# A two-layer hybrid trunk in one program: squares summed on VectorE, the norms' odd tiles on VectorE, three waits placed elsewhere

## The chip, the cores and the metric

The kernel runs on one core of a Trainium2 chip. The metric is the device time of one execution in microseconds (us). The core has TensorE (PE, matrix products), VectorE (DVE), ScalarE (ACT), GpSimd (POOL) and SyncE (SP, which here only issues loads). Each engine works through its own instruction list in order, and engines wait for each other on semaphores.

## The reference

Two layers over 512 latent and 256 context tokens of width 1024, in float32. Each layer:

```
h      = rms_norm(x) * gain * (1 + scale) + shift          # scale, shift from silu(c) @ w_mod
qa,ka,va,qb,kb,vb,qkv,z,beta,a,gate = split(h @ w_in)
o_a    = attention(rms(qa), rms(ka), va)                   # with rotary columns
o_b    = neighbourhood_attention(qb, kb, vb)               # 8 x 16 window, learned bias
o_c    = gated_delta(conv(qkv), beta, a) * silu(z)         # both directions, chunks of 64 tokens
x      = x + gate_m * ((sum_n sigmoid(gate_n) * (o_n @ w_branch[n])) @ w_out)
x      = x + gate_f * (square(relu(h2 @ w_ffn1)) @ w_ffn2) # h2: norm and modulation again
```

The second layer keeps only the latent tokens after its token mixers. A last rms_norm ends the trunk.

## The kernel before

Activations lie transposed: channels on the 128 partitions, tokens along the free dimension, so x is `xT`, eight tiles (k = 0 to 7) of 128 channels by 768 tokens (512 where only latent tokens count). Every product of float32 data is done as three TensorE passes over a high and a low half (`hh`, `hl` for activations, `wh`, `wl` for weights; lines 423 to 425). SP loads weight slots into a ring of three; `high` (line 1001, ACT) copies a slot to `wh`, and `split` (line 1686, POOL) makes `wl`. `high(l, name, i)` works two slots ahead, and before each slot it waits until the product that used the place three slots earlier has been filled. PSUM is four buffers used in turn by `take`: the fourth product after one needs that one's buffer emptied.

The program is one hand-written order for each engine. In a layer it goes: norm "mix"; twelve conv projections and z; the delta rule (six steps `s`, two directions `d`, each with five steps of a matrix power series, whose product is written L554); q and k heads (six `j`, each a square, its sum by TensorE at L808, root, reciprocal, and two projections `x = 2j, 2j+1` of the neighbourhood branch between); attention; 24 gate and branch products `x` whose sum is merged into `mT`; eight `out` products; norm "ffn"; eight groups of ff1 and ff2. After the second layer there is a norm "fin". So five norms run in all: three over 768 tokens (mix of both layers, ffn of the first) and two over 512 (ffn of the second, fin).

A norm has two parts.

- *The sum of squares.* ACT squares tile k (L957) into one of two buffers, and TensorE multiplies it by a matrix of ones and adds up over k (L600): eight products, each buffer free for the next square when its product has run. ACT then takes the root (L959) and DVE the reciprocal (L1260).
- *Scaling.* For even k, DVE multiplies x by gain and reciprocal root into `ht` (L1282, one piece for latent and one for context tokens), ACT adds the shift and rounds to `hh` (L976), DVE writes the remainder `hl` (L1291). For odd k, POOL multiplies x by the root (L1696), ACT applies gain and shift (L981) and rounds (L984), and DVE writes `hl` (L1296). `ht` has three buffers. In "fin" POOL takes tiles 1, 3 and 5, and DVE the rest.

In the residual stretch ahead of a norm, DVE adds product j into `xT[:, j]` (`residual`, L1621) and so frees the product's PSUM buffer. ACT's list there is: all `high` calls of the stretch first, then the norm's root table and its squares.

The delta state's zeroing (L1460) waits for `z_saved`, the store of z to DRAM that shares the place, and stands on DVE ahead of the first decay (L1468) and masked matrices (L1476, L1480); L1487 makes the first X out of them, and L1502 and L1506 empty the products of the power series.

After gate and branch product 23, DVE multiplies (L1603) and adds (L1606); ACT rounds all eight tiles of `mT` (L1226) and DVE writes their remainders (L1613), tile by tile ahead of the first `out` product.

Of the kernel before, what the change touches and what calls it, by code (L numbers as in the profile page):

```python
# [15 lines left out]
F32 = mybir.dt.float32  # L16
# [90 lines left out]
def program(nc, a, out, x_store, skew, bias_rows, z_store, book):  # L107
    book["final"] = book.get("final", False)
    with ExitStack() as ctx:
# [108 lines left out]
        def want_out(l, t):  # L218
            return l == 0 or t < LT

# [189 lines left out]
        def _(pe):  # L410
# [184 lines left out]
            def norm(l, which, ntok):  # L595
                ps = take(pe, "ss", l, which)
                for k in range(KC):
                    pe.wait_ge(*act_done.at("sq", l, which, k))
                    for t0, t1 in ((0, LAT), (LAT, TOK))[:1 if ntok == LAT else 2]:
                        last = mm(ps[:, t0:t1], ones, sq_n[:, k % 2, t0:t1], start=(k == 0), stop=(k == KC - 1))  # L600
                    if k < KC - 1:
                        last.then_inc(*pe_done.mark("ss", l, which, k))
                last.then_inc(*filled("ss", l, which))
# [338 lines left out]
        def _(act):  # L942
            A = nc.scalar.activation

            def norm(l, which, ntok):
                act.wait_ge(*dve_done.at("eps"))
                A(small[:, 62:63], eps[:, 0:1], ACT.Sqrt)
                for k in range(KC):

                    if l == 0 and which == "mix":  # L950
                        if k == 0:
                            act.wait_ge(*read("x", TT - 1))
                    else:
# [18 lines left out]
                for k in range(KC):  # L972
                    if k % 2 == 0:
                        act.wait_ge(*dve_done.at("scaled", l, which, k))
                        for t0, t1, c in spans(ntok):
                            A(hh[:, k, t0:t1], ht[:, k % 3, t0:t1], ACT.Identity, bias=modcs[:, l, 24 * w + k, c:c + 1])\  # L976
                                .then_inc(*act_done.mark("hhi", l, which, k))
                    else:
                        act.wait_ge(*pool_done.at("hx", l, which, k))
                        for t0, t1, c in spans(ntok):  # L980
                            A(ht[:, k % 3, t0:t1], ht[:, k % 3, t0:t1], ACT.Identity, scale=gains[:, l, w, k, c:c + 1],  # L981
                              bias=modcs[:, l, 24 * w + k, c:c + 1]).then_inc(*act_done.mark("aff", l, which, k))
                        act.wait_ge(*act_done.at("aff", l, which, k))
                        A(hh[:, k, 0:ntok], ht[:, k % 3, 0:ntok], ACT.Copy).then_inc(*act_done.mark("hhi", l, which, k))  # L984
# [24 lines left out]
            for l in range(DEPTH):  # L1009
# [164 lines left out]
                for j in range(6):  # L1174
# [3 lines left out]
                    A(asq[:, 0:n], qk[:, j, 0:n], ACT.Square).then_inc(*act_done.mark("asq", l, j))  # L1178
                    act.wait_ge(*full("ass", l, j))
# [43 lines left out]
                for k in range(KC):  # L1223

                    act.wait_ge(*dve_done.at("merge", l, 23))
# [28 lines left out]
        def _(dve):  # L1254
            V = nc.vector

            def inverse_root(l, which, ntok):
# [4 lines left out]
            def norm(l, which, ntok):  # L1262
# [13 lines left out]
                for k in range(KC + 1):  # L1276
                    if k < KC and k % 2 == 0:

                        if k >= 3:
                            dve.wait_ge(*dve_done.at("h", l, which, k - 3))  # L1280
# [90 lines left out]
            for l in range(DEPTH):  # L1371
                nt = TOK if l == 0 else LAT
                pcol, modc = pcols[:, l, :], modcs[:, l, :, :]
                if l == 0:
# [4 lines left out]

                    inverse_root(0, "mix", TOK)  # L1380
# [78 lines left out]
                dve.wait_ge(*z_saved.at(l))  # L1459
                V.memset(state[:, 0, :, :], 0.0).then_inc(*dve_done.mark("S0", l))  # L1460
# [135 lines left out]
                for k in range(4):  # L1596
                    branch_low(l, 2, k)
                for x in range(24):
                    n, dc = divmod(x, 8)
                    dve.wait_ge(*full("br", l, x))  # L1600
# [10 lines left out]
                for k in range(KC):  # L1611
                    dve.wait_ge(*act_done.at("mhi", l, k))
                    V.tensor_tensor(hl[:, k, 0:nt], mT[:, k, 0:nt], hh[:, k, 0:nt].bitcast(F32), ALU.subtract)\  # L1613
                        .then_inc(*dve_done.mark("mlo", l, k))
# [35 lines left out]
        def _(pool):  # L1650
# [39 lines left out]
            def normed(l, which, ntok, ks=range(1, KC, 2)):  # L1690

                pool.wait_ge(*dve_done.at("rs", l, which))
                for k in ks:
                    if k >= 3 and which != "fin":
                        pool.wait_ge(*dve_done.at("h", l, which, k - 3))
# [5 lines left out]
            for l in range(DEPTH):  # L1701
# [8 lines left out]
                if l == 0:  # L1710
                    normed(l, "mix", TOK, (1,))
                for p in range(2):
                    split(l, "c", c_order[p])
                normed(l, "mix", TOK, (3, 5, 7) if l == 0 else (1, 3, 5, 7))

                pool.wait_ge(*pool_done.at("hx", l, "mix", KC - 1))
# [190 lines left out]
                normed(l, "ffn", nt)  # L1907
# [38 lines left out]
```

## Time and profile before

| | us |
|---|---|
| median of three runs | 3248.0 |
| lowest, highest | 3242.76, 3248.76 |
| the profiled execution's own time | 3252.78 |
| its span | 3251.0 |
| PE busy | 2994.1 |
| DVE busy | 1231.6 |
| ACT busy | 1060.5 |
| POOL busy | 1071.1 |

The mean granted TensorE clock is 0.968 of full speed.

The profile describes one execution; a row gives start, duration, engine, source line and tiles. "R" is the one large scratch tensor in which most work buffers lie, `xT`, `ht` and the squares among them. Busy shares are means over stages with different limits, so what a stage waits for has to be read at its own place in the trace.

### The profile page before, as it was taken

Reading aid. Unit: us, or ns where it says so; the run is one execution under the profiler, and the core shown is the slowest. Engines: PE = TensorE matmul, PEld = TensorE weight load, DVE = VectorE, ACT = ScalarE, POOL = GpSimd, SP = SyncE. Lnnn points to the kernel's source line nnn. Section 1 sums busy time; section 2 is a strip of 40 time slices with the busy share of each in tenths; the row PEclk is TensorE's granted clock in tenths of the full one; section 3 lists DMA queues with packets and bytes.
Section 4 is the critical chain, followed back from the end, with each engine's and each line's share of the span. In section 5 each row is a group of like instructions: output and inputs, shape, how many; then the busy total and the mean of one; then the engine's idle time right before and its main releaser. Section 6 shows DMA issues by size and latency. Waiting matters only on the chain.

```text
span 3251.0 us, 57566 instructions
## 1 busy us (share of the span) xinstructions
PE 2994.1 (92%) x24931; PEld 2500.1 (77%) x24931; DVE 1231.6 (38%) x1754; ACT 1060.5 (33%) x1770; POOL 1071.1 (33%) x720
## 2 busy tenths in 40 slices
PE   5997888998889999799999979999999899989998
PEld 3886777776668888688888868788777688768886
DVE  3773433244541212322222258654235621232223
ACT  3542222225542112322221235433225532243222
POOL 3233344220313333222222322355330344444442
PEclk7998999999999999899999989999999999999999
DMA  6115453110002232121222221100310034323331
GB/s 229 53 35 176 149 184 107 54 44 7 11 23 59 67 99 72 33 66 60 64 65 65 61 69 52 47 3 4 84 49 11 11 91 133 101 71 93 96 97 59
DMA packets 303690, 231.93 MB, mean 71 GB/s; under 512 B 16784, under 2 KB 275280, under 8 KB 302544
## 3 DMA queue, kind: packets, MB, share of 16 engines
q1 hardware_dynamic: 297360, 204.58, 21.0%
q0 software_dynamic: 3776, 17.91, 1.5%
q10 hardware_dynamic: 2304, 5.77, 0.5%
q8 instruction: 198, 3.24, 0.4%
q14 instruction: 52, 0.43, 0.0%
HBM read 217.22 MB, written 11.98 MB: 71 GB/s over the span
## 4 chain that ended last, share of the span: by engine, by line
PE 79%; DVE 10%; issue 5%; ACT 4%; DMA 1%; POOL 1%; ACTq 0%; DVEq 0%; POOLq 0%
PE ps L423 20%; PE ps L424 20%; PE ps L425 20%; PE ps L554 5%; DVE stat L1316 2%; PE ps L508 2%; PE ps L529 2%; DVE R L1428 1%; PE ps L546 1%; DVE R L1282 1%; PE ps L435 1%; PE ps L600 1%; PE ps L770 1%; PE ps L720 1%; ACT R L878 1%
## 5 line engine op out<-in xcount | busy, mean ns | idle before, releaser
L1686 POOL TENSOR_TENSOR wl<-wring,wh 128x1024 fp32r<-128x1024 f32 (+1 forms) x312 | 721.1, 2314 | 1339.8 <-ACT wh L1001 1339.8
L423 PE MATMUL ps<-hh,wh 128*128 128x512 f32 (+1 forms) x2560 | 923.4, 361 | 73.7 <-DVE hl L1291 41.2
L424 PE MATMUL ps<-hl,wh 128*128 128x512 f32 (+1 forms) x2560 | 905.1, 354 | 0.0
L425 PE MATMUL ps<-hh,wl 128*128 128x512 f32 (+1 forms) x2560 | 904.3, 353 | 0.0
L423 PEld LDWEIGHTS ps<-hh,wh 128*128 128x128 f32 x2560 | 489.9, 191 | 163.1 <-issue 57.6
L424 PEld LDWEIGHTS ps<-hl,wh 128*128 128x128 f32 x2560 | 491.0, 192 | 68.2 <-issue 5.1
L425 PEld LDWEIGHTS ps<-hh,wl 128*128 128x128 f32 x2560 | 490.2, 191 | 66.2
L1001 ACT ACTIVATE wh<-wring 128x1024 fp32r<-128x1024 f32 (+1 forms) x312 | 307.7, 987 | 522.8 <-PE ps L425 497.8
L1621 DVE SCALAR_TENSOR_TENSOR R<-ps,modcs,R 128x512 f32<-128x512 f32 x216 | 136.3, 659 | 388.4 <-PE ps L425 387.5
L424 PE MATMUL ps<-fl,wh 128*128 128x512 f32 (+1 forms) x768 | 274.8, 358 | 0.0
L425 PE MATMUL ps<-fh,wl 128*128 128x512 f32 (+1 forms) x768 | 274.5, 357 | 0.0
L423 PE MATMUL ps<-fh,wh 128*128 128x512 f32 (+1 forms) x768 | 274.3, 357 | 0.0
L554 PE MATMUL ps<-R 64*64 64x64 f32 x5376 | 184.8, 224 | 23.9 <-issue 7.9
L554 PEld LDWEIGHTS ps<-R 64*64 64x64 f32 x5376 | 171.1, 138 | 39.9 <-issue 21.8
L1603 DVE TENSOR_TENSOR R<-ps,R 128x768 f32<-128x768 f32 (+1 forms) x48 | 39.6, 824 | 410.1 <-PE ps L425 410.1
L1635 DVE TENSOR_TENSOR R<-R 128x768 f32<-128x768 f32 (+1 forms) x64 | 53.9, 841 | 363.0 <-ACT R L1239 363.0
L878 ACT ACTIVATE R<-ps,stat 128x768 f32<-128x768 f32 (+2 forms) x160 | 116.0, 728 | 143.8 <-DVE stat L1316 139.8
L423 PEld LDWEIGHTS ps<-fh,wh 128*128 128x128 f32 x768 | 144.7, 188 | 23.7
L424 PEld LDWEIGHTS ps<-fl,wh 128*128 128x128 f32 x768 | 144.5, 188 | 23.3
L425 PEld LDWEIGHTS ps<-fh,wl 128*128 128x128 f32 x768 | 144.4, 188 | 23.3
L529 PE MATMUL ps<-R 128*64 128x128 f32 x1408 | 95.2, 279 | 38.2 <-DVE R L1337 29.3
L1239 ACT ACTIVATE R<-ps 128x768 f32<-128x768 f32 (+1 forms) x64 | 45.2, 706 | 255.1 <-PE ps L425 198.3
(236 smaller groups left out, 3775.6 us busy)
## 6 DMA issues: line engine op xcount, KB each, us to landing
wring<-in_w_ffn SPq DMA_DIRECT2D x128, 512.0 KB, 3.9
wring<-in_w_in SPq DMA_DIRECT2D x116, 512.0 KB, 3.8
wboth<-in_w_mod SPq DMA_DIRECT2D x80, 512.0 KB, 6.4
wring<-in_w_branch SPq DMA_DIRECT2D x48, 256.0 KB, 2.7
wring<-in_w_out SPq DMA_DIRECT2D x16, 512.0 KB, 4.2
x_store<-R POOLq DMA_DIRECT2D x2, 3072.0 KB, 9.0
R<-x_store POOLq DMA_DIRECT2D x2, 3072.0 KB, 11.6
R<-in_w_mod SPq DMA_DIRECT2D x7, 512.0 KB, 13.4
```

The source lines that it names most:

```text
L423: mm(ps[:, t0:t1], ahk, rh[:, k, t0:t1], start=(k == 0), stop=False)
L424: mm(ps[:, t0:t1], ahk, rl[:, k, t0:t1], start=False, stop=False)
L425: last = mm(ps[:, t0:t1], alk, rh[:, k, t0:t1], start=False, stop=(k == kn - 1))
L508: last = mm(ps[u][:, c0:c0 + n1 - n0], q[lo:lo + HD, t * P:t * P + P], k[lo:lo + HD, n0:n1], start=True, stop=True)
L529: mm(PS[3][HD * u:HD * u + HD, 512:512 + P], vt[b][:, c0:c0 + HD], probT[br][:, u, b, :], start=(b == 0), stop=(b == nk - 1))
L554: last = mm(out[lo:lo + HALF, h * HALF:h * HALF + HALF], left[lo:lo + HALF, h, :], right[lo:lo + HALF, h, :], start=True, stop=True)
L878: nc.scalar.activation(prob[br][p % 2][:, u, 0:n], score_ps(l, p)[u][:, 0:n], ACT.Exp, bias=stat[:, sl, 0:1], accum_out=stat[:, sl, 1:2])\
L1001: A(slot_view(wh, n % NSPL, *slot), w, ACT.Copy).then_inc(*act_done.mark("whi", *slot))
L1316: V.tensor_reduce(stat[:, sl, 0:1], ps[:, 0:n], AX.X, ALU.max, negate=True)\
L1621: V.scalar_tensor_tensor(out=xT[:, j, t0:t1], in0=pair(*key)[:, t0:t1], scalar=modc[:, gate + j, c:c + 1], in1=xT[:, j, t0:t1], op0=ALU.mu ...
L1635: V.tensor_tensor(f, f, f, ALU.mult).then_inc(*dve_done.mark("fsq", l, j))
L1686: G.tensor_tensor(slot_view(wl, n % NSPL, l, name, i), w, slot_view(wh, n % NSPL, l, name, i).bitcast(F32), ALU.subtract)\
```

## The change

Six edits, all of them in what stands on which engine and in which order:

1. The squares of tiles 0 to 5 are added up on VectorE (`square_sum`, five additions per norm), each put behind a residual; TensorE multiplies by ones only this sum and tiles 6 and 7. The squares of tiles 1 to 5 and 7 lie in the three `ht` buffers.
2. In "mix" and "ffn" VectorE multiplies the odd tiles too (L1299 of the new file), and POOL none.
3. The delta state's zeroing moves behind the first masked matrices.
4. The square of head j+1 stands on ACT between the two projections of head j, where it stood behind both (`head_square`).
5. ACT rounds tile k of `mT` once merge 16+k is done, and no longer waits for merge 23 in all eight.
6. DVE writes the remainder of tile 0 of `mT` ahead of merge 23.

```diff
+        def square_home(k):
+            return sq_n[:, k // 6, :] if k in (0, 6) else ht[:, k % 3, :]
...
             def norm(l, which, ntok):                         # TensorE
-                for k in range(KC):
-                    pe.wait_ge(*act_done.at("sq", l, which, k))
+                for k in (KC - 3, KC - 2, KC - 1):
+                    pe.wait_ge(*(dve_done.at("sum", l, which, k) if k == KC - 3 else act_done.at("sq", l, which, k)))
+                    sq = sq_n[:, 0, :] if k == KC - 3 else square_home(k)
...
-                    if k >= 2:                                # ScalarE
-                        act.wait_ge(*pe_done.at("ss", l, which, k - 2))
-                    A(sq_n[:, k % 2, 0:ntok], xT[:, k, 0:ntok], ACT.Square).then_inc(*act_done.mark("sq", l, which, k))
+                    if k in (4, 5, 7):
+                        act.wait_ge(*dve_done.at("sum", l, which, k - 3))
+                    A(square_home(k)[:, 0:ntok], xT[:, k, 0:ntok], ACT.Square).then_inc(*act_done.mark("sq", l, which, k))
...
-                        act.wait_ge(*pool_done.at("hx", l, which, k))
+                        act.wait_ge(*dve_done.at("scaled", l, which, k))
...
+                head_square(l, 0)
+                for j in range(6):
...
+                        if x == 2 * j + 1 and j < 5:
+                            head_square(l, j + 1)
...
-                    act.wait_ge(*dve_done.at("merge", l, 23))
+                    act.wait_ge(*full("gate", l, 23))
+                    act.wait_ge(*dve_done.at("merge", l, 16 + k))
...
+            def square_sum(l, which, ntok, k):                # VectorE
+                dve.wait_ge(*act_done.at("sq", l, which, k))
+                dve.wait_ge(*(dve_done.at("sum", l, which, k - 1) if k > 1 else act_done.at("sq", l, which, 0)))
+                V.tensor_tensor(sq_n[:, 0, 0:ntok], sq_n[:, 0, 0:ntok], square_home(k)[:, 0:ntok], ALU.add)\
+                    .then_inc(*dve_done.mark("sum", l, which, k))
...
+                    if k < KC and k % 2:
+                        V.tensor_tensor(ht[:, k % 3, 0:ntok], xT[:, k, 0:ntok], rs_n[:, 0:ntok], ALU.mult)\
+                            .then_inc(*dve_done.mark("scaled", l, which, k))
...
-                dve.wait_ge(*z_saved.at(l))
-                V.memset(state[:, 0, :, :], 0.0).then_inc(*dve_done.mark("S0", l))
...
                 for d in range(2):
                     delta_keys(l, 0, d)
+                dve.wait_ge(*z_saved.at(l))
+                V.memset(state[:, 0, :, :], 0.0).then_inc(*dve_done.mark("S0", l))
...
                     residual(("out", l, j), j, 16)
+                    if 2 <= j < KC - 1:
+                        square_sum(l, "ffn", nt, j - 1)
...
                             residual(("ff2", l, g - 1, j), j, 40)
+                            if g == NG and 2 <= j < KC - 1:
+                                after = (1, "mix", TOK) if l == 0 else (DEPTH, "fin", LAT)
+                                square_sum(*after, j - 1)
...
-                normed(l, "ffn", nt)                          # GpSimd
```

VectorE at the first layer's `out` products, before. Each residual is two pieces, 512 and 256 tokens; ps_full is the product it waits for, and the rows shown are residuals 2 to 4:

```order
L1621 SCALAR_TENSOR_TENSOR R<-ps,modcs,R 128x512 [waits ps_full2]
L1621 SCALAR_TENSOR_TENSOR R<-ps,modcs,R 128x256
L1621 SCALAR_TENSOR_TENSOR R<-ps,modcs,R 128x512 [waits ps_full3]
L1621 SCALAR_TENSOR_TENSOR R<-ps,modcs,R 128x256
L1621 SCALAR_TENSOR_TENSOR R<-ps,modcs,R 128x512 [waits ps_full0]
```

The same place in the changed kernel, where L1653 is the residual and L1272 the addition of a square:

```order
L1653 SCALAR_TENSOR_TENSOR R<-ps,modcs,R 128x512 [waits ps_full2]
L1653 SCALAR_TENSOR_TENSOR R<-ps,modcs,R 128x256
L1272 TENSOR_TENSOR R<-R 128x768 [waits act_done]
L1653 SCALAR_TENSOR_TENSOR R<-ps,modcs,R 128x512 [waits ps_full3]
L1653 SCALAR_TENSOR_TENSOR R<-ps,modcs,R 128x256
L1272 TENSOR_TENSOR R<-R 128x768 [waits dve_done,act_done]
L1653 SCALAR_TENSOR_TENSOR R<-ps,modcs,R 128x512 [waits ps_full0]
```

An addition that waits for ACT's squares now stands between residual 2 and residual 3, and one behind each residual up to the sixth.

ScalarE at the same place in the changed kernel (L1004 is `high`, L950 the root table, L960 a square); the list before has the same rows in the same order, with other waits on the squares:

```order
L1004 ACTIVATE wh<-wring 128x1024 [waits ps_full1,w_full2]
L1004 ACTIVATE wh<-wring 128x1024 [waits ps_full2,w_full0]
L950 ACT_TABLE_LOAD
L950 ACTIVATE small<-eps 128x1 [waits dve_done]
L960 ACTIVATE R<-R 128x768 [waits ps_free0]
L960 ACTIVATE R<-R 128x768 [waits ps_free1]
```

The last L1004 waits for ps_full2, which is `out` product 6; the squares stand behind it as they did.

VectorE at the start of the first layer's delta rule, before:

```order
L1457 TENSOR_TENSOR gex<-gex,bg 128x6x8 [waits act_done]
L1460 MEMSET R 128x1024 [waits z_saved]
L1468 TENSOR_TENSOR R<-ps,gcs 128x256 [waits ps_full0]
L1468 TENSOR_TENSOR R<-ps,gcs 128x256 [waits ps_full1]
L1476 TENSOR_TENSOR R<-ps,R 128x256 [waits ps_full2,act_done]
L1480 TENSOR_TENSOR R<-R 128x256 [waits pool_done,ps_free2]
```

The same place in the changed kernel:

```order
L1481 TENSOR_TENSOR gex<-gex,bg 128x6x8 [waits act_done]
L1490 TENSOR_TENSOR R<-ps,gcs 128x256 [waits ps_full0]
L1490 TENSOR_TENSOR R<-ps,gcs 128x256 [waits ps_full1]
L1498 TENSOR_TENSOR R<-ps,R 128x256 [waits ps_full2,act_done]
L1502 TENSOR_TENSOR R<-R 128x256 [waits pool_done,ps_free2]
L1498 TENSOR_TENSOR R<-ps,R 128x256 [waits ps_full2,act_done]
L1502 TENSOR_TENSOR R<-R 128x256 [waits pool_done,ps_free2]
L1517 MEMSET R 128x1024 [waits z_saved]
L1509 TENSOR_TENSOR R<-R,cst 128x256 [waits ps_free0] x2
```

Six instructions pass the zeroing; the first X (L1509) stays behind it.

## Rows read from the trace of the kernel before

**Rows 1.** The page: shares of the last-ending chain by engine.

```profile
PE 79%; DVE 10%; issue 5%; ACT 4%; DMA 1%; POOL 1%; ACTq 0%; DVEq 0%; POOLq 0%
```

**Rows 2.** Timeline, PE, head squares: start, us, instruction, count, idle before.

```profile
632.85 1.56 PE L808 MATMUL ps<-R,cst 128*128 128x512 f32 x4 [1.69 <-ACT R L1178]
...
2352.14 1.12 PE L808 MATMUL ps<-R,cst 128*128 128x512 f32 x2 [1.26 <-ACT R L1178]
```

**Rows 3.** The chain that ended last, norm "ffn" of layer 0.

```profile
1316.98 10.34 PE ps L600 x32
...
1333.32 2.80 DVE R L1282 x2
...
1355.29 0.80 PE ps L423
```

**Rows 4.** Timeline of DVE: the first norm, then that of rows 3.

```profile
50.44 7.55 DVE L1282 SCALAR_TENSOR_TENSOR R<-R,gains 128x512 f32<-128x512 f32 x2
...
1337.36 1.14 DVE L1291 SCALAR_TENSOR_TENSOR hl<-R,modcs,hh 128x512 fp32r<-128x512 f32 x2 [1.25 <-ACT hh L976]
1338.42 2.70 DVE L1282 SCALAR_TENSOR_TENSOR R<-R,gains 128x512 f32<-128x512 f32 x2
1341.04 0.94 DVE L1296 TENSOR_TENSOR hl<-R,hh 128x768 fp32r<-128x768 f32 x1
```

**Rows 5.** Timeline of POOL at the same two places.

```profile
52.39 4.64 POOL L1686 TENSOR_TENSOR wl<-wring,wh 128x1024 fp32r<-128x1024 f32 x2
...
1338.58 2.26 POOL L1696 TENSOR_TENSOR R<-R 128x768 f32<-128x768 f32 x1 [3.42 <-DVE hl L1291]
```

**Rows 6.** Timeline of ACT, norm "ffn" of layer 0, from its last weight copy.

```profile
1308.73 1.06 ACT L1001 ACTIVATE wh<-wring 128x1024 fp32r<-128x1024 f32 x1 [7.28 <-PE ps L425]
...
1311.22 1.56 ACT L957 ACTIVATE R<-R 128x768 f32<-128x768 f32 x2
...
1336.20 1.12 ACT L976 ACTIVATE hh<-R,modcs 128x512 fp32r<-128x512 f32 x2 [7.90 <-DVE R L1282]
1337.23 1.29 ACT L981 ACTIVATE R<-R,modcs,gains 128x512 f32<-128x512 f32 x2
1338.55 0.84 ACT L984 ACTIVATE hh<-R 128x768 fp32r<-128x768 f32 x1
```

**Rows 7.** The chain, norm "ffn" of layer 1, to the first product behind it.

```profile
2846.71 7.45 PE ps L600 x16
...
2858.35 1.86 DVE R L1282
...
2871.93 0.50 PE ps L423
```

**Rows 8.** The chain at the start of the delta rule, layer 0.

```profile
249.12 8.75 issue
...
258.10 0.91 DVE R L1460
...
264.45 5.18 PE ps L554 x96
```

**Rows 9.** The same chain in layer 1.

```profile
2076.47 2.72 issue
...
2085.73 3.37 PE ps L554 x64
```

**Rows 10.** The chain from the last branch product to the first `out` product, layer 0.

```profile
1245.47 0.97 DVE R L1606
...
1248.44 0.47 PE ps L423
```

**Rows 11.** Windows there: length; busy time (instructions) of PE, PEld, DVE, ACT, POOL; granted clock; DMA.

```profile
1248.00:1252.00 4.00, 3.56 (x9) 2.76 (x10) 4.00 (x6) 4.00 (x7) 0.00 (x0) 0.61 0.00 0
```

**Rows 12.** Timeline of ACT: first squares of the last "mix" and of "fin".

```profile
1881.46 1.56 ACT L957 ACTIVATE R<-R 128x768 f32<-128x768 f32 x2
...
3205.80 1.13 ACT L957 ACTIVATE R<-R 128x512 f32<-128x512 f32 x2
```

More of the change, by code:

```diff
@@ L596, in norm @@
                 ps = take(pe, "ss", l, which)
-                for k in range(KC):
-                    pe.wait_ge(*act_done.at("sq", l, which, k))
+                for k in (KC - 3, KC - 2, KC - 1):
+                    pe.wait_ge(*(dve_done.at("sum", l, which, k) if k == KC - 3 else act_done.at("sq", l, which, k)))
+                    sq = sq_n[:, 0, :] if k == KC - 3 else square_home(k)
                     for t0, t1 in ((0, LAT), (LAT, TOK))[:1 if ntok == LAT else 2]:
-                        last = mm(ps[:, t0:t1], ones, sq_n[:, k % 2, t0:t1], start=(k == 0), stop=(k == KC - 1))
-                    if k < KC - 1:
-                        last.then_inc(*pe_done.mark("ss", l, which, k))
+                        last = mm(ps[:, t0:t1], ones, sq[:, t0:t1], start=(k == KC - 3), stop=(k == KC - 1))
                 last.then_inc(*filled("ss", l, which))
@@ L1173, in _, with head_square @@
                 act.wait_ge(*read("va", l))
-                for j in range(6):
+                def head_square(l, j):
                     n = TOK if j >= 4 else nt
@@ L1276, in norm @@
                 for k in range(KC + 1):
[L1277 to L1280 removed]
+                    if k < KC and k >= 3:
+                        dve.wait_ge(*dve_done.at("h", l, which, k - 3))
+                    if k < KC and k % 2:
+                        V.tensor_tensor(ht[:, k % 3, 0:ntok], xT[:, k, 0:ntok], rs_n[:, 0:ntok], ALU.mult)\
+                            .then_inc(*dve_done.mark("scaled", l, which, k))
+                    elif k < KC:
                         for t0, t1, c in spans(ntok):
@@ L1378, in params @@
                         dve.wait_ge(*read("params", ll))
+                    for k in range(1, KC - 2):
+                        square_sum(0, "mix", TOK, k)
                     inverse_root(0, "mix", TOK)
@@ L1597, in _, with merged_low @@
                     branch_low(l, 2, k)
+                def merged_low(l, k):
+                    dve.wait_ge(*act_done.at("mhi", l, k))
+                    V.tensor_tensor(hl[:, k, 0:nt], mT[:, k, 0:nt], hh[:, k, 0:nt].bitcast(F32), ALU.subtract)\
+                        .then_inc(*dve_done.mark("mlo", l, k))
                 for x in range(24):
                     n, dc = divmod(x, 8)
+                    if x == 23:
+                        dve.wait_ge(*full("gate", l, 23))
+                        merged_low(l, 0)
                     dve.wait_ge(*full("br", l, x))
@@ L1610, in _ @@
                         branch_low(l, (x - 1) // 4, (x - 1) % 4)
[L1611 to L1614, printed above, removed]
+                for k in range(1, KC):
+                    merged_low(l, k)
                 def residual(key, j, gate):
@@ L1688, in split, with normed @@
                     .then_inc(*pool_done.mark("wlo", l, name, i))
-            def normed(l, which, ntok, ks=range(1, KC, 2)):
+            def normed(l, which, ntok, ks):
                 pool.wait_ge(*dve_done.at("rs", l, which))
                 for k in ks:
-                    if k >= 3 and which != "fin":
-                        pool.wait_ge(*dve_done.at("h", l, which, k - 3))
                     G.tensor_tensor(ht[:, k % 3, 0:ntok], xT[:, k, 0:ntok], rs_n[:, 0:ntok], ALU.mult)\
@@ L1709, in _ @@
                     load_params(DEPTH)
-                if l == 0:
-                    normed(l, "mix", TOK, (1,))
                 for p in range(2):
                     split(l, "c", c_order[p])
-                normed(l, "mix", TOK, (3, 5, 7) if l == 0 else (1, 3, 5, 7))
-                pool.wait_ge(*pool_done.at("hx", l, "mix", KC - 1))
+                pool.wait_ge(*dve_done.at("scaled", l, "mix", KC - 1))
                 pool.dma_start(x_store, R[:, XT0:RN]).then_inc(*spilled.mark(l, by=16))
```

1 line of the change is left out of this document (added).

## The prediction

> **What bounds the kernel now.** I read the page first, then the chain that ended last. TensorE holds 79% of that chain [rows 1]. The rest are places where TensorE stands still behind other engines, so an edit is worth what it takes off such a place. I then took the chain and each engine's timeline at every place that the diff touches. There are four kinds.
>
> - The head squares: PE is idle 1.69 us ahead of L808 for 768 tokens and 1.26 us for 512, each time released by ACT's square [rows 2]. The first kind stands five times in layer 0 and twice in layer 1, the second three times; the first head of each layer waits for something else.
> - The norms. In "ffn" of layer 0 the products with ones take 10.34 us, then come root and reciprocal, and 21.97 us pass from the first scaling (1333.32) to the first product (1355.29) [rows 3].
> - The start of the delta rule: 8.75 us of waiting in layer 0 and 2.72 us in layer 1, all of it DVE ahead of its zeroing, then a chain through decays and matrices up to the power series [rows 8, 9].
> - The step to `out`: merge 23 is added at 1245.47 and the first product starts at 1248.44 [rows 10].
>
> **The change part by part.**
>
> *Head squares.* Head j+1's square now stands ahead of ACT's copies of projection 2j+1, so it is done some 8 us before PE asks. ACT's weight copy behind it comes 0.84 us later for a weight needed two products on. Gain 5 x 1.69 + 3 x 1.26 + 2 x 1.69 = **15.6 us**. It is hidden by a whole projection, so I see no lower value than 14.
>
> *Odd tiles on DVE.* DVE's first scaling pass takes 2.70 us while POOL multiplies, and its other pass of the same shape 1.14 [rows 4]; POOL's multiplication runs 2.26 us just then [rows 5]. So DVE's pass waits for POOL's and then runs. With POOL out I price DVE's four passes for two tiles at 1.14, 0.94, 1.14, 0.94, less 0.08 of overlap each, 3.84 us a pair. ACT needs 1.12, 1.29 and 0.84 [rows 6], 3.25 a pair, which fits beside it. Walking both lists from the first scaling: 15.4 us of DVE, waits for ACT of 0.4 at tile 0, 0.2 at tiles 3 and 5 each, 1.2 at tile 7, end at 17.5. Before it was 21.9. Gain 4.4 us, in three norms. Of this the first scaling gives 1.7 (2.80 to 1.14) and the rest of the walk 2.7. The first norm has one thing more: its first scaling took 7.55 us [rows 4], ending just behind POOL's multiplication (which took 1.8 there) and two weight splits of 4.64 [rows 5]. The splits stay, the multiplication goes, so the first scaling gives 1.8, and the norm 4.5. In layer 1's "ffn" (512 tokens) first scaling to first product took 13.6 us [rows 7]; the same walk gives 12.0, gain 1.5. Sum 4.5 + 4.4 + 4.4 + 1.5 = **14.8 us**. The store of x leaves POOL earlier within the norm, but less so than the norm shrinks; conv has over 5 us of slack there.
>
> The Trainium skill ("SBUF — State Buffer", section "SBUF: two separate sides") says that VectorE with two SBUF inputs and GpSimd reading SBUF exclude each other for a whole instruction. The 7.55 us agree. By that rule the new additions can also be blocked, and block POOL's splits; this gives a rival below.
>
> *Zeroing.* Decays and matrices need nothing of z. In layer 0 they now run inside the 8.75 us of waiting, and the first power product too. When z's store has landed, the zeroing runs at 258.10 (0.91) and then X's start (0.8, from two passes), so X's products start at 259.8. Before, PE restarted at 264.45 with 5.18 us of power and X products [rows 8]; a third of them, X's 1.7 us, still lies behind. They end at 261.5 for 269.6: 8.1 us sooner at most. I take 7.5, since ACT's copies of the power products queue behind z as well. If the power products are not done ahead, it is 264.45 - 259.8 = 4.7. In layer 1 the chain from 2076.47 to PE at 2085.73 is 9.26 us [rows 9], of which waiting (2.72) and zeroing (0.91 and its start, 0.2) are 3.8; the key products come 0.6 later than the decays want them, but PE is idle for less and its clock stays up. I take 3.9, bounds 3 and 4.5. Sum **11.4 us**.
>
> *The step to `out`.* Tiles 0 to 6 are rounded while branch product 23 runs. Behind merge 23 DVE starts on tile 1 at 1246.4, PE on tile 1 at 1247.5, where it had begun tile 0 at 1248.44 [rows 10] and tile 1 at 1249.7. DVE's pace (0.87 a tile, from 0.94 with overlap [rows 4]) stays ahead of PE, whose clock is low at first (0.61 in the next 4 us [rows 11]), so PE keeps 1.7 of the 2.2. Layer 1 alike, 2.0. Sum **3.7 us**.
>
> *Squares summed ahead.* TensorE runs 3 of 8 products: 10.34/8 = 1.29 us each, so up to 6.4 are saved [rows 3], 7.45/8 = 0.93 each for 512 tokens, up to 4.6 [rows 7]. But the first addition stands on DVE between residuals 2 and 3. Residual 3 frees the PSUM buffer of product 7. And ACT's squares stand behind all its weight copies, of which the last waits for product 6.
>
> - "ffn", layer 0: that copy runs at 1308.73, just when PE would start product 7. The first two squares end at 1312.78 [rows 6], then the addition (0.95) and residual 3 (1.14): product 7 starts at 1315.0, **6.4 us late**. That stall is also enough for the clock: behind the wait ahead of `out`, over 3 us [rows 10], the granted clock was 0.61 over 4 us [rows 11], the high level (2.4 GHz) in the smaller part of it and 1.2 GHz in the rest, and 4 us at 0.61 of full speed lose 1.6 to 1.8 us. Product 7 ends at 1325.1, three products with ones at 1329.0; before, 1327.3. Loss 1.7.
> - "ffn", layer 1: the same with 512 tokens. Stall 5.2, clock 1.8, saved 4.6: loss 2.3.
> - "mix", layer 1: the squares start at 1881.46, when product 5 has just ended [rows 12], and end at 1883.0; a POOL split there holds the addition to about 1884.9. Product 7 is 0.7 to 1.5 late, and DVE (2.0 for a residual and an addition) becomes the bound, its last addition at 1892.8. Gain 2.0, bounds -1.5 and 3.2.
> - "fin": the squares start at 3205.80 [rows 12], ahead of residual 2, and no product waits. Gain five products of 0.93: 4.7 us.
> - First norm: all squares follow the last transpose, and the products with ones begin cold 5 us later. Gain 1.2.
>
> Sum 1.2 - 1.7 + 2.0 - 2.3 + 4.7 = **3.9 us**, of 23 that the removed products alone suggest.
>
> **Sum.** 15.6 + 14.8 + 11.4 + 3.7 + 3.9 = 49.4 us. Against the profiled execution (3252.8) that is 3203.4. It lies 4.8 above the median of the runs, 3248.0, and against the median I predict **3198.6 us**. A measurement of this kernel tells 0.2% (6.5 us) from no change.
>
> **Rivals.**
>
> - *The additions cost no stall* (a). If PE did not have to wait for residual 3, both "ffn" would keep 6.4 and 4.6, and "mix" of layer 1 its 6.4: 3.9 + 8.1 + 6.9 + 4.4 = 23.3 for the squares, time 3179. For it: the additions' own work, 0.95 us, is small. Against: the order of the two lists, and the last weight copy at 1308.73 [rows 6]. Chance 0.06.
> - *Parts are given back in contention* (b). Additions and POOL's splits hold each other up around each stall and in "mix" of layer 1 (some 5 us over four norms at 2.4 us a split), and the start of the delta rule keeps only the 4.7 and 3 us bounds (3.7 less): 3207. With "mix" of layer 1 at its lower bound 3.5 more: 3211. The exclusion rule cited above points this way. For it: the 7.55 us [rows 4]. Against: at the `out` products ACT copies, and so POOL splits, one weight in 8.34 us (7.28 and 1.06 [rows 6]). Chance 0.15.
> - *Slower* (c). The new stalls of 6.4 and 5.2 us leave the clock at the low level, not for 4 us but through the stage behind. Each 8.3 us product would cost 8.3 more, and the gain is gone from six products in all; with ten it is 3280. Against: the low level was over within 4 us at the step to `out` [rows 11], behind a wait of the same kind, and the mean granted clock is 0.968. Chance 0.03. The Trainium skill ("TensorE: Matmul & The Clock Gate", "Part 1: The HAM clock gate") says that sustained activity releases the throttle, which speaks against this rival.
> - *The edits don't do what they say* (d), because the heads' and norms' waits are each replaced at once by another one just behind (a weight split for the head squares, PE's own low clock for the norms): within 6.5 us of 3248. Chance 0.03.
> - My forecast: 0.73, its own range 3190 to 3207.
>
> **How the numbers follow.** The range from 3181 to 3213 leaves out (a)'s end, (c), (d) and the tails of the rest, some 2 in 10. Faster by over 0.2%: the forecast, (a) and (b), 0.94; within: 0.03; slower: 0.03.
>
> **What would show it.** No idle time ahead of the heads' product with blocks for j of 1 and up; DVE's first passes at 1.14 us in the norms, and first scaling to first product of 17.5 us; DVE's zeroing behind L1502 and only it behind the store; PE idle 6 us ahead of `out` product 7 of layer 0 and 5 us in layer 1, and DVE waiting at its first addition for ACT's square at that time; three products with ones per norm where there were eight. I am wrong if PE runs through product 7, if the clock stays low there, or if the delta rule's first modulation product waits for its weights.

## The result, and the profile after

| us | before | after |
|---|---|---|
| median | 3245.4 | 3217.5 |
| lowest, highest | 3242.8, 3248.8 | 3215.1, 3220.0 |
| profiled execution | 3252.8 | 3215.6 |
| PE busy | 2994.1 | 2966.8 |
| DVE busy | 1231.6 | 1249.9 |
| mean granted clock | 0.968 | 0.971 |

Before was timed four times here; its median of 3248.0 in the prediction was that of three. The ratio is 0.9905 (0.9888 to 0.9922): faster, as predicted, but 27.9 us by the medians (30.8 by the ratio) where 49.4 were predicted, and 4.5 us outside the range. The two profiled executions lie 37.2 apart. To see where, I cut both at the same TensorE instructions (starts in the two timelines; the last column holds the prediction's terms):

```
stretch                                                     before   after   change  predicted
first norm, first conv product to its context half           80.18   76.79    -3.4     -5.7
conv, up to z                                                 81.94   81.80    -0.1      0
z, delta rule up to the first X product in layer 0           105.80   99.10    -6.7     -7.5
six delta steps, layer 0                                     311.96  313.75    +1.8      0
up to the heads                                               30.52   28.95    -1.6      0
heads, layer 0                                               106.84   96.39   -10.4     -8.4
attention and branch products, layer 0                       500.53  499.57    -1.0      0
last branch products and out product 0                        40.67   43.93    +3.3     -1.7
out products 1 to 7, norm ffn, first ff1 products            110.12  108.90    -1.2     -2.7
ff1, ff2, norm mix and first conv product of layer 1         562.61  557.77    -4.8     -6.4
conv, layer 1                                                 80.73   80.99    +0.3      0
z, delta rule up to the first X products in layer 1           76.45   71.62    -4.8     -3.9
six delta steps, layer 1                                     246.64  246.59     0.0      0
heads, layer 1                                                93.15   85.45    -7.7     -7.2
attention and branch products, layer 1                       335.54  336.86    +1.3      0
last branch products, out products 0 and 1, layer 1           50.22   52.67    +2.5     -2.0
rest of out, norm ffn, first ff1 product, layer 1             58.82   59.97    +1.2     +0.8
ff1, ff2, fin                                                378.22  372.69    -5.5     -4.7
```

Of the 12.2 us that are missing inside the profiles, 9.4 stand at the step to `out`, where 3.7 of gain had been predicted and 5.7 were lost. The other 6.7 us of the miss (18.9 in all) are no place in the kernel: I had taken off 4.8 because before's profiled execution lay that far above its median, and expected the same of after, whose profiled execution lies 1.9 below its median. One execution each of the later runs e9 and e14 took 5988 and 6766 us; they are in no ratio, median or spread given below.

**The step to `out`.** Timelines of before (DVE, ACT, POOL):

```profile
1247.34 7.04 DVE L1613 TENSOR_TENSOR hl<-R,hh 128x768 fp32r<-128x768 f32 x8 [0.91 <-ACT hh L1226]
...
1252.35 1.99 ACT L1001 ACTIVATE wh<-wring 128x1024 fp32r<-128x1024 f32 x2
...
1253.53 5.46 POOL L1686 TENSOR_TENSOR wl<-wring,wh 128x1024 fp32r<-128x1024 f32 x2 [17.37 <-ACT wh L1001]
```

The changed kernel's timeline of DVE, for a wide and a narrow window:

```profile
1224.93 10.50 DVE L1625 TENSOR_TENSOR hl<-R,hh 128x768 fp32r<-128x768 f32 x7
...
1227.53 6.16 DVE L1625 TENSOR_TENSOR hl<-R,hh 128x768 fp32r<-128x768 f32 x2
```

of ACT and POOL at the same place:

```profile
1225.85 1.99 ACT L1004 ACTIVATE wh<-wring 128x1024 fp32r<-128x1024 f32 x2
...
1227.04 5.83 POOL L1723 TENSOR_TENSOR wl<-wring,wh 128x1024 fp32r<-128x1024 f32 x2 [12.29 <-ACT wh L1004]
```

and its windows (length; busy time and instructions of PE, PEld, DVE, ACT, POOL; granted clock; DMA), to be read against [rows 11]:

```profile
1223.00:1227.00 4.00, 1.72 (x7) 0.88 (x6) 3.91 (x5) 3.69 (x6) 0.00 (x0) 0.97 0.01 2
1227.00:1231.00 4.00, 3.02 (x7) 1.92 (x8) 4.00 (x3) 0.84 (x1) 3.96 (x2) 0.60 0.01 2
1231.00:1235.00 4.00, 1.93 (x6) 1.26 (x6) 4.00 (x3) 0.00 (x0) 1.87 (x1) 0.83 0.64 185
```

Seven remainders took 10.50 us where eight took 7.04 before. Five were normal and two took 3.1 each, those two that met a weight split of POOL. ACT has rounded seven tiles ahead of merge 23, so its weight copies come at 1225.85, 0.8 us behind the end of that merge, where they came 5.9 behind it (1252.35), and the splits (1253.53) met only the last remainder. POOL's splits come with them. TensorE waits for three of the remainders (2.29, 0.98 and 2.07 us) and is idle for 5.3 of the 12 us in the windows. In layer 1 the seven took 8.6 us, eight had taken 4.9.

**The stall of product 7.** Timeline of ACT, DVE and PE in layer 0:

```profile
1290.59 1.06 ACT L1004 ACTIVATE wh<-wring 128x1024 fp32r<-128x1024 f32 x1 [7.28 <-PE ps L429]
...
1293.06 2.29 ACT L960 ACTIVATE R<-R 128x768 f32<-128x768 f32 x3
...
1294.65 0.96 DVE L1272 TENSOR_TENSOR R<-R 128x768 f32<-128x768 f32 x1 [36.34 <-ACT R L960]
1295.53 1.14 DVE L1653 SCALAR_TENSOR_TENSOR R<-ps,modcs,R 128x512 f32<-128x512 f32 x2
...
1296.81 0.76 PE L427 MATMUL ps<-hh,wh 128*128 128x512 f32 x1 [6.32 <-DVE R L1653]
```

DVE was idle for 36.34 us ahead of its first addition, and TensorE waits 6.3 us for residual 3 behind it. This is the predicted stall, in size too. In all nine traces that have it, product 7 starts 14.8 us behind product 6 where 8.3 are normal, and then takes 9.7 to 11.1 us for 8.2: the granted clock is 0.50 in the first 4 us behind the stall in the changed kernel. That costs 1.5 to 2.9 us, where the prediction had 1.6 to 1.8.

**The norms.** Timeline of DVE in "ffn" of layer 0 (for [rows 3, 4]):

```profile
1317.66 1.15 DVE L1304 SCALAR_TENSOR_TENSOR R<-R,gains 128x512 f32<-128x512 f32 x2
1318.72 0.95 DVE L1299 TENSOR_TENSOR R<-R 128x768 f32<-128x768 f32 x1
...
1334.40 0.96 DVE L1318 TENSOR_TENSOR hl<-R,hh 128x768 fp32r<-128x768 f32 x1 [1.19 <-ACT hh L987]
```

The first pass takes 1.15 for 2.80, and from the first scaling to the end of the last remainder 17.7 us pass where the walk gave 17.5.

**Heads and zeroing.** PE's waits in the heads of layer 0 (us in total, times, longest), where five of 1.69 had stood besides the first:

```profile
PE ps L811 <- ACT R L1182: 1.8, 1, 1.8
```

and the start of the delta rule, DVE and PE (for [rows 8]):

```profile
250.05 0.64 DVE L1502 TENSOR_TENSOR R<-R 128x256 f32<-128x256 f32 x1
255.25 0.91 DVE L1517 MEMSET R<- 128x1024 f32 x1 [4.57 <-DMA z_store<-R]
256.08 1.22 DVE L1509 TENSOR_TENSOR R<-R,cst 128x256 f32<-128x256 f32 x2
...
252.18 2.08 PE L558 MATMUL ps<-R 64*64 64x64 f32 x64 [0.76 <-ACT R L1125]
257.69 1.97 PE L558 MATMUL ps<-R 64*64 64x64 f32 x32 [3.43 <-DVE R L1526]
```

Both masked matrices, the 32 matmuls that turn them and the 64 of the first power product now lie inside the wait for z's store, as predicted; the 32 of the first X product stand behind it.

### The profile page after: what moved, and what is told of

It is laid out like the page before. It is cut to its first block and busy times, and to the rows that moved or that the text cites. A ratio compares the mean times of both kernels' runs of the same rounds, so it can differ in the third digit from the quotient of the medians.

```text
span 3213.8 us, 57461 instructions
## 1 busy us (share of the span) xinstructions
PE 2966.8 (92%) x24851; PEld 2485.8 (77%) x24851; DVE 1249.9 (39%) x1795; ACT 1059.7 (33%) x1770; POOL 1039.5 (32%) x704
## 3 DMA queue, kind: packets, MB, share of 16 engines
q1 hardware_dynamic: 297360, 204.58, 21.2%
## 5 line engine op out<-in xcount | busy, mean ns | idle before, releaser
L429 PEld LDWEIGHTS ps<-hh,wl 128*128 128x128 f32 x2560 | 492.1, 192 | 66.2
L1004 ACT ACTIVATE wh<-wring 128x1024 fp32r<-128x1024 f32 (+1 forms) x312 | 307.6, 987 | 540.2 <-PE ps L429 512.2
L1653 DVE SCALAR_TENSOR_TENSOR R<-ps,modcs,R 128x512 f32<-128x512 f32 x216 | 136.2, 658 | 318.7 <-PE ps L429 317.8
L533 PEld LDWEIGHTS ps<-R 128*64 128x64 f32 x1408 | 78.2, 139 | 66.9 <-ACT R L895 46.5
## 6 DMA issues: line engine op xcount, KB each, us to landing
R<-x_store POOLq DMA_DIRECT2D x2, 3072.0 KB, 11.2
```

The source lines that it names most:

```text
L429: last = mm(ps[:, t0:t1], alk, rh[:, k, t0:t1], start=False, stop=(k == kn - 1))
L533: mm(PS[3][HD * u:HD * u + HD, 512:512 + P], vt[b][:, c0:c0 + HD], probT[br][:, u, b, :], start=(b == 0), stop=(b == nk - 1))
L1004: A(slot_view(wh, n % NSPL, *slot), w, ACT.Copy).then_inc(*act_done.mark("whi", *slot))
L1653: V.scalar_tensor_tensor(out=xT[:, j, t0:t1], in0=pair(*key)[:, t0:t1], scalar=modc[:, gate + j, c:c + 1], in1=xT[:, j, t0:t1], op0=ALU.mu ...
```

## The experiments

Each kernel was timed 4 to 12 times, and before beside it on the same chip. e2, e6, e7 and e8 shared one chip, e1, e3, e4 and e5 another, e9 to e12 a third, the last four a fourth.

### Each edit alone

The kernel before with edit 4, 3, 2, 1 alone, or 5 and 6 together, each as in the diff above and nothing else.

```diff
# e1_heads
+                        if x == 2 * j + 1 and j < 5:
+                            head_square(l, j + 1)
# e3_zero: the memset behind delta_keys
# e5_odd: L1299; GpSimd multiplies in fin only
# e4_squares: square_sum, square_home, three products with ones
# e2_step
-                    act.wait_ge(*dve_done.at("merge", l, 23))
+                    act.wait_ge(*full("gate", l, 23))
+                    act.wait_ge(*dve_done.at("merge", l, 16 + k))
...
+                    if x == 23:
+                        dve.wait_ge(*full("gate", l, 23))
+                        merged_low(l, 0)
```

> The kernel before with edit 4 alone (the next head's square between the two projections). Forecast's term: 15.6 us faster. The lag of the traces of the whole change at these places was 9.8 in layer 0 and 7.8 in layer 1, 17.6. Rival: part is given back behind the heads: 10 or less.

> The kernel before with edit 3 alone (the delta state's zeroing behind the first masked matrices). Forecast's term: 11.4 us faster (7.5 and 3.9). In the whole change the lag grew by 7 us in layer 0 and 4 to 5 in layer 1, but shrank again by some 3 us within the delta steps of layer 0, where TensorE's granted clock was 0.68 in one stretch. If that belongs to the edit, 7 to 9; if it is chance, 11.

> The kernel before with edit 2 alone (odd tiles of the norms multiplied on VectorE). Forecast's term: 14.8 us faster (4.5, 4.4, 4.4, 1.5). By the lags of the whole change the norms gave 4.8, 4.2, 4.7 and 1.1, but about 2 us of three of them were lost at the first product behind the norm, which starts with a colder clock: 9 to 10. If this loss is not the edit's, 14.8.

> The kernel before with edit 1 alone (five additions on VectorE, three products with ones). Forecast's term: 3.9 us faster (+1.2 first norm, -1.7 and -2.3 in the two ffn, +2.0 mix of layer 1, +4.7 fin). By the lags of the traces of the whole change: -1.1, -2.5 to -4.8 in each ffn, +2.6, +5: from 1 us faster to 3 slower.

> The kernel before with edits 5 and 6 alone (ScalarE rounds tile k of mT after merge 16+k, VectorE writes tile 0's remainder ahead of merge 23). My forecast had it 3.7 us faster. Theory of contention: ScalarE's two weight copies for the second and third out products now come while VectorE still writes remainders, so GpSimd's weight splits (2.4 us each, two of them) run against the remainders; two of the seven remainders took 3.1 us in the changed kernel where none took over 0.96 before, and the lag between the two traces shrank by some 3 us net at this place in each layer. So 4 to 7 us slower than before, VectorE's seven remainders at 10.5 us in layer 0 and 8.6 in layer 1. Rival, the clock: TensorE starts on one tile, waits, and runs at the low level for longer; then slower by as much, but with remainders of 0.95 us.

| edit | predicted | ratio | us by the ratio | us in its own stretches |
|---|---|---|---|---|
| 4, heads | -15.6 | 0.9946 (0.9925 to 0.9967) | -17.5 (-24 to -11) | -8.8 and -9.1 |
| 3, zeroing | -11.4 | 0.9969 (0.9954 to 0.9985) | -10.1 (-15 to -5) | -7.4 and -5.0 |
| 2, odd tiles | -14.8 | 0.9977 (0.9962 to 0.9993) | -7.5 (-12 to -2) | -9.2 to -11.2 |
| 1, sums | -3.9 | 1.0008 (0.9996 to 1.0021) | +2.6 (-1 to +7) | -2.3 |
| 5 and 6, step | -3.7 | 1.0034 (1.0021 to 1.0048) | +11.0 (+7 to +16) | +4.6 and +3.7 |

Heads and zeroing are what they were priced at, within their intervals. (The two ends for the odd tiles come from taking the stretches of e1, e2 and e3, which lack this edit too, or those of before, as the base: behind the norm "ffn" of layer 0 alone these differ by 1.2 us. For the same reason the +4.6 is +3.3 against e1, e3 and e5.) Added up, the rows give -21.5 us by whole times, with some 12 either way (an estimate from the five intervals), and -33 to -35 in the stretches; the whole change gives -30.8 by its ratio and -37.2 between its profiles. So no large part of the miss lies in how the edits act on each other. Edits 5 and 6 make the kernel slower by themselves. VectorE's instruction groups of e2_step at the first step to `out` (count, busy us, mean ns):

```profile
L1602 DVE TENSOR_TENSOR hl<-R,hh 128x768 fp32r<-128x768 f32 x7 | 10.5, 1569 | 0.0
```

That is the figure expected from contention, and not 0.95 us each as the clock rival says. And with edit 1 alone PE's wait for a residual ahead of product 7, layer 0 and then 1, is there just as in the whole change:

```profile
PE ps L427 <- DVE R L1633: 6.3, 1, 6.3
...
PE ps L427 <- DVE R L1633: 5.2, 1, 5.2
```

In stretches edit 1 costs 1.5 and 3.3 us in the two "ffn" (predicted 1.7 and 2.3), brings 2.3 in "mix" of layer 1 (2.0) and 4.9 in "fin" (4.7), and nothing in the first norm (1.2).

### The step to `out`

```diff
# e6_nostep, e16_nostep_again: the changed kernel without edits 5 and 6
# e7_gate, e14_gate_again: the changed kernel with, on GpSimd,
                 for i in range(8):
+                    if i == 1:
+                        pool.wait_ge(*dve_done.at("mlo", l, KC - 1))
                     split(l, "out", i)
# e12_nostep_gate, e15_nostep_gate_again: both
```

> The changed kernel without edits 5 and 6 (rounding and remainders of mT as before). By the contention theory and by the clock rival, 4 to 7 us faster than the changed kernel (3217.5), so near 3212; by my forecast's term it would be 3.7 us slower, 3221.

> The changed kernel with one more wait: GpSimd's split of the second out product's weights waits for VectorE's last remainder of mT. Contention theory: the seven remainders take 6.2 us in layer 0 and 4.3 in layer 1 where they took 10.5 and 8.6, the weight is split 2.4 us behind the last of them, in time for product 1, and 4.3 us come back in each layer: 3209, 8.6 faster than the changed kernel and 2 to 3 faster than without edits 5 and 6. Clock rival: remainders shorter, but TensorE is at the low level anyway: within 2 us of 3217.5.

> A control for the wait: the changed kernel without edits 5 and 6, but with GpSimd's second out split behind VectorE's last remainder. Here ScalarE's copies come late anyway and the split would start within 1 us of the last remainder, so the wait alone should do nothing: the time of the kernel without edits 5 and 6 (0.9895 of before, within 3 us). The difference to the kernel that has the edits and the wait (0.9873) is then what edits 5 and 6 are worth once the collision is gone: 3 to 8 us. If the wait by itself brings the gain, this one is at 0.9873 as well.

> The changed kernel with GpSimd's second out split behind VectorE's last remainder, once more, now on one chip with its control. By the stretches of the traces (last 52 gate and branch steps of TensorE and out product 0) edits 5 and 6 with this wait are worth 1.7 us in layer 0 and 1.8 in layer 1 against the order before, so this kernel is some 3.5 us faster than the control. If the control's median of 3203 was right and the trace misleads, no difference or slower.

> The control once more: without edits 5 and 6, with the wait. By the traces the wait does nothing here, so this kernel and the one without edits 5 and 6 and without the wait agree within 3 us; by the medians of two chips the wait alone brought 9 us.

> Without edits 5 and 6 and without the wait, once more, on the control's chip: within 3 us of the control if the wait alone does nothing, 9 us slower if it does.

```
                          ratio to before               last branch products to the end of out product 0 (layer 0), 1 (layer 1)
before                                                    40.67    50.22
changed kernel            0.9905                          43.93    52.67
e10, the same again       0.9899 (0.9879 to 0.9919)       43.91    52.63
e6, without 5 and 6       0.9895 (0.9879 to 0.9910)       41.94    50.23
e7, with the wait         0.9873 (0.9861 to 0.9886)       38.97    48.44
e12, wait, without 5, 6   0.9868 (0.9852 to 0.9884)       40.60    50.25
e16, e6 again             0.9891 (0.9870 to 0.9912)       40.64    50.22
e14, e7 again             0.9887 (0.9865 to 0.9908)       38.94    48.42
e15, e12 again            0.9892 (0.9872 to 0.9912)       41.94    50.24
```

e7's timeline, DVE and then POOL:

```profile
1223.86 6.16 DVE L1625 TENSOR_TENSOR hl<-R,hh 128x768 fp32r<-128x768 f32 x7
...
1230.10 4.75 POOL L1723 TENSOR_TENSOR wl<-wring,wh 128x1024 fp32r<-128x1024 f32 x2 [16.43 <-DVE hl L1625]
```

With the splits behind the remainders, seven take 6.16 us, the splits themselves 4.75 for 5.83, and the step is 5.0 and 4.2 us shorter than in the changed kernel, 1.7 and 1.8 shorter than before. That is what the forecast had priced (1.7 and 2.0) without the collision; e14 repeats both lengths. Of the 5.0 us in layer 0, 3.05 are two waits of TensorE for a remainder (0.98 and 2.07), which e7 no longer has. The rest goes with the clock: it is 0.83 in the changed kernel's last window above, and 1.00 in e7's from 1230 to 1234. So the low clock takes part, but as a consequence: the clock rival, which had it low anyway and expected nothing of the wait, falls. In layer 1 the wait has a price too: TensorE stands still 1.0 us for a split that now comes later.

e6 itself was 3 us faster than the changed kernel by the ratios, inside the noise, where 4 to 7 were expected; in its stretches it is 2.0 and 2.4 shorter. By whole times the control e12 missed: 9 us faster than e6, where its expectation had them within 3. In layer 0 it is 1.3 us shorter at the step, but the repeats have it the other way round (e15 with the wait 41.94, e16 without it 40.64), so kernels without edits 5 and 6 take one of two lengths there, wait or not. Repeated on one chip, e14, e15 and e16 are within 0.05% of each other. So no effect of the wait alone is seen, and the 9 us were the spread between executions and chips. That edits 5 and 6 with the wait bring 1.7 to 3.0 us in layer 0 and 1.8 in layer 1 is seen in the stretches only; by whole times it is 1 to 2 us with more than 5 us of uncertainty, so e14's expectation of 3.5 is not shown there.

### Where the additions stand

```diff
# e8_late, in "ffn", and alike behind ff2
                     residual(("out", l, j), j, 16)
-                    if 2 <= j < KC - 1:
-                        square_sum(l, "ffn", nt, j - 1)
+                    if j == KC - 2:
+                        for k in range(1, KC - 2):
+                            square_sum(l, "ffn", nt, k)
# e9_both: e8_late and e7_gate
# e11_splitfirst: e9_both, and in layer 0
+                for p in range(2):
+                    split(l, "c", c_order[p])
                 if l == 0:
                     load_params(DEPTH)
-                for p in range(2):
-                    split(l, "c", c_order[p])
# e13_ffnlate: e11, the late additions in "ffn" only
```

> The changed kernel with the five additions of squares all behind residual 6 instead of one behind each residual from 2 on. Theory of the order: residual 3 no longer stands behind ScalarE's squares, so out product 7 starts at once in both layers (6.5 and 5.5 us of waiting gone) and its clock stays high (2.3 and 1.6), with what the norms lost against before (2.5 and 3.2) turned into the saved five products of 6.4 and 4.6: 8.9 and 7.8 us; in mix of layer 1 up to 3.8, in fin nothing. Sum 20: near 3198. Rival: five additions in a row (4.8 us) behind residual 6, and square 7 behind the fourth of them, delay the products with ones, so that only half comes back: near 3207.

> The changed kernel with both remedies: the additions behind residual 6, and GpSimd's second out split behind VectorE's last remainder. The two places are apart. If both causes are right their gains add: from 0.9905 of before to 0.9877 for the one and 0.9873 for the other, so to about 0.9845, 3193 to 3196 us. If both gave back the same thing (a clock that stays up after either), no better than 0.987.

> The changed kernel as it is, once more, on the chip of the remedies: 0.9905 of before, 3214 to 3218; it gives the remedies their base on the same chip.

> The kernel with both remedies, and in layer 0 GpSimd's first two weight splits ahead of its loads of the last parameters, for which it waits some 4 us. In the changed kernel the first scaling of the first norm took 5.81 us beside the two splits (4.66). If a split and a two-input VectorE instruction on SBUF exclude each other, the first scaling falls to about 1.2 us, the first product comes 4 us earlier and the time is 4 us less than with both remedies. If the 5.81 has another cause, no change.

> The kernel with both remedies and the earlier splits, but the additions stand behind residual 6 only in ffn; in mix of layer 1 and in fin they stand behind each residual, as in the changed kernel. There the products are 4.2 and 2.8 us apart, and five additions in a row (4.8 and 3.4 us) don't fit between the last two. Theory: fin's end gets back the 1.9 to 3.6 us that the row cost, mix of layer 1 is equal either way: 2 to 3 us faster than the kernel with everything behind residual 6. Rival: the 1.9 to 3.6 us were a matter of the clock: no difference.

e8_late came to 3205.1 us, ratio 0.9877 (0.9863 to 0.9891), near the rival's 3207 and not the 3198 of my theory. Timeline of DVE, "ffn" of layer 0 and then the end of ff2 ahead of "fin":

```profile
1293.48 5.21 DVE L1272 TENSOR_TENSOR R<-R 128x768 f32<-128x768 f32 x5 [3.00 <-ACT R L960]
1298.61 1.14 DVE L1653 SCALAR_TENSOR_TENSOR R<-ps,modcs,R 128x512 f32<-128x512 f32 x2
...
3173.34 0.75 DVE L1653 SCALAR_TENSOR_TENSOR R<-ps,modcs,R 128x512 f32<-128x512 f32 x1 [2.06 <-PE ps L429]
3174.01 3.87 DVE L1272 TENSOR_TENSOR R<-R 128x512 f32<-128x512 f32 x5
3177.79 0.75 DVE L1653 SCALAR_TENSOR_TENSOR R<-ps,modcs,R 128x512 f32<-128x512 f32 x1
```

Product 7 of `out` now starts at once in both layers. From the start of `out` product 1 to that of the first ff1 product of layer 0 it is 73.6 us, for 81.1 in the changed kernel; in layer 1 (out product 1 to the second ff1 product) 62.3 for 66.2. Of the expected 8.9 and 7.8 that is 7.5 and 3.8. The rest is lost behind product 7, as the rival had it: from its last matmul to the first ff1 product it is 15.3 us for 13.9 in layer 0, and 13.9 for 9.8 in layer 1. In "mix" of layer 1 nothing is gained (537.9 both), and "fin" loses: ff2 products are 2.8 us apart there, five additions in a row take 3.87, and the residual of product 7 stands behind them. From ff1 to fin it is 366.1 us for 362.5. e13, with the row in "ffn" only, has 362.5 again, but its ratio, 0.9844 (0.9822 to 0.9867), is no better than e9's or e11's; 2 us are below what these runs tell.

e9_both is at 0.9844 (0.9830 to 0.9858), 3196.8 us. The two remedies add up (0.9845 expected), so they act at two places. e10, the changed kernel on the same chip, is at 0.9899.

e11: timelines of DVE and POOL in the first norm, the changed kernel's two rows ahead of e11's two.

```profile
49.96 5.81 DVE L1304 SCALAR_TENSOR_TENSOR R<-R,gains 128x512 f32<-128x512 f32 x2
...
50.16 4.66 POOL L1723 TENSOR_TENSOR wl<-wring,wh 128x1024 fp32r<-128x1024 f32 x2
```

```profile
50.65 1.15 DVE L1304 SCALAR_TENSOR_TENSOR R<-R,gains 128x512 f32<-128x512 f32 x2
...
44.66 4.69 POOL L1725 TENSOR_TENSOR wl<-wring,wh 128x1024 fp32r<-128x1024 f32 x2
```

A third row of e11's DVE stands amid these splits:

```profile
46.05 0.17 DVE L1371 TENSOR_TENSOR modcs<-ps,pcols 128x8 f32<-128x8 f32 x1 [2.46 <-PE ps L449]
```

With the two splits out of its way the first scaling falls from 5.81 to 1.15 us, and the time from PE's first modulation product to its first conv product from 21.2 to 18.1. The whole is 3195.4 us, 0.9838 (0.9824 to 0.9853), 1.4 better than e9 where 4 were expected. e9, e11 and e13 can't be told apart; each is some 50 us faster than before and 20 faster than the change.

## Why the prediction was wrong

**The failed step is "DVE's pace (0.87 a tile ...) stays ahead of PE".** The pace of VectorE's remainders was taken from a row in which POOL was still, and ACT's copies were not followed to where the removed wait let them go. ACT, freed from merge 23, copies two weights during the remainders; POOL splits them (2.4 us each) and blocks two remainders for 2.2 us each. Predicted -3.7, measured +5.7 in the profiles (+4.4 against e6); e7 takes the collision out and nothing else, and gets 5.0 and 4.2 back. This is the largest part of the 12.2 us inside the profiles, and without it the time would be some 3208 us (an estimate, 3217.5 less 9.4), inside the range. Rival (b), contention, was right in kind, but I had placed it at the additions and argued against it with the splits' spacing at later `out` products.

There the Trainium skill's rule ("SBUF — State Buffer", section "SBUF: two separate sides"), which the prediction applied to the first scaling and the additions, holds just as much: a VectorE instruction with two SBUF inputs and a GpSimd instruction that reads SBUF shut each other out for a whole instruction. The traces agree: 3.1 us is one remainder (0.94) behind most of one split (2.40); and in e11 VectorE's small additions out of PSUM (0.17 us each) ran beside the splits undelayed: 0.17 us is also what they took clear of them.

**Heads and zeroing: right.** 15.6 and 11.4 predicted; 17.5 and 10.1 by whole times alone, 17.8 and 12.3 in the stretches.

**Squares summed ahead: the mechanism was right, as was the size of each stall** (6.4 and 5.2 predicted, 6.3 and 5.2 of TensorE's waiting both in the change and alone). The term "First norm: gain 1.2" was not there: the time to the first modulation product is 36.0 to 37.9 us in all kernels with either order. Layer 1's "ffn" lost 3.3 for 2.3. Rival (a) falls with the stalls, and (c) with the clock, which is back at 1.00 from 1304.8 us on, 8 us behind the stall of layer 0.

**Odd tiles on DVE: the walk was right to 0.2 us, the term 4 to 6 us too large by the stretches of e5** (14.8 for 9.2 to 11.2; 7.5, with 5 either way, by whole times). What the norm gains at its last tile is not all kept. In the first norm the eighth tile's product starts 4.8 us sooner (72.38 for 77.18), but TensorE is then still at the low clock level, and the context half goes at 0.41 us a matmul where it is 0.28 later in the trace; at the sixth tile of the context half 3.4 are left (80.18, 76.79).

```profile
73.82 0.41 PE L427 MATMUL ps<-hh,wh 128*128 128x256 f32 x1
```

**The base.** A single profiled execution was corrected by the difference to a median of three. The six delta steps of layer 0 have the same instruction lists in all eighteen profiles, and take 302 to 318 us there; the heads of layer 0 take 96.4 or 98.1 with the new order. Such jumps are not the edits', and they set the uncertainty of every whole time here: 3 to 22 us between the fastest and slowest execution of one kernel.

What stays open: why these stretches jump. The granted clock differs in them between executions (0.68 in 16 us of one delta step of the changed kernel, 1.00 in the same step of before), but no experiment was made on it.

## What to carry to other kernels

When a wait is removed from an engine, follow everything that stands behind it on that engine, and who is released by that in turn: here the rounding was rightly moved, and two weight copies and two splits came along and took more than it brought. Take an instruction's duration from a row in which the same neighbours run as will run after the change. An addition of 0.95 us costs TensorE 6 where it must itself wait for another engine and stands ahead of the release of a PSUM buffer; put it behind the last release that TensorE needs, if the row of additions is shorter than a product.

## What the hardware showed that I had not expected

- A weight split on POOL and a two-input DVE pass on SBUF cost each other whole instructions even when each is short: 0.94 becomes 3.1 us, and two splits go from 4.75 to 5.83.
- Stretches with identical instruction lists take one of a few lengths, 1.6 us apart: 28.95 or 30.5 us ahead of the heads, 96.4 or 98.1 in them. Where two traces of one kernel can differ so, a stretch must be seen in more than one trace before a microsecond is put down to an edit.
